# Second mixer: query and forget transposes and all decay levels moved two units up, key copies taken ahead of the exponentials

## The reference, cut to what matters

```python
proj = h @ w_in[i]
da_q, da_k, da_v, hg_q, hg_zf, hg_zb, hg_v, hg_g = split(proj)
# differential attention, 4 heads, two score maps per head
a = softmax(einsum('bqhmd,bkhmd->bhmqk', q * scale, k))
w = a[:, :, 0] - lam * a[:, :, 1]
o_da = rmsnorm_2(einsum('bhqk,bkhe->bqhe', w, v), subln_g) * (1 - lambda_init)
# recurrence, forwards and backwards, 4 heads of 128
log_f = log(lb + (1 - lb) * sigmoid(z))
k_in = (1 - lb) * sigmoid(-z)
state = exp(sum of log_f) * state + k_in^T v ; y = q state
o_hg = rmsnorm_2(y_forward + y_backward, norm_g) * silu(g)
x = x + concat([o_da, o_hg]) @ w_out[i]
```

## Time and profile before

| | us |
|---|---|
| median of 3 runs | 959.13 |
| lowest and highest | 958.48, 961.9 |
| the profiled execution's own time | 959.75 |
| its span | 957.9 |
| TensorE busy | 916.5 (96%) |
| VectorE, ScalarE, GpSimd busy | 593.1, 492.6, 115.7 |
| mean granted TensorE clock | 0.988 of full speed |

### The profile page before, as it was taken

How to read it: one execution, slowest core, us unless ns; L and a number is a source line. 1 busy time by engine, 2 the same in 40 slices (tenths; PEclk the granted TensorE clock), 3 DMA queues, 4 the chain that set the end, 5 groups by cost and what they waited for, 6 DMA issues and landing times.

```text
span 957.9 us, 14230 instructions
## 1 busy us (share of the span) xinstructions
PE 916.5 (96%) x4869; PEld 772.0 (81%) x4869; DVE 593.1 (62%) x882; ACT 492.6 (51%) x729; POOL 115.7 (12%) x107
## 2 busy tenths in 40 slices
PE   7999999999999899999999999997999999999996
PEld 5788888888787677888888878786778999999875
DVE  5655555568756546654555557887666666757664
ACT  6444444465754546444444456554636544545463
POOL 5210000020033202000000021632002000000020
PEclk9999999999999999999999999998999999999998
DMA  9796666447722223655555627441245665555611
GB/s 312 205 266 201 216 191 217 141 129 242 241 68 70 85 69 129 220 186 192 191 186 186 190 75 263 128 140 62 66 129 169 198 196 180 180 192 173 196 45 44
DMA packets 122040, 157.43 MB, mean 164 GB/s; under 512 B 10047, under 2 KB 83011, under 8 KB 122000
## 3 DMA queue, kind: packets, MB, share of 16 engines
q1 hardware_dynamic: 119648, 151.65, 49.6%
q0 software_dynamic: 1904, 4.65, 1.9%
q10 hardware_dynamic: 448, 0.59, 0.2%
HBM read 155.79 MB, written 1.07 MB: 164 GB/s over the span
## 4 chain that ended last, share of the span: by engine, by line
PE 86%; DVE 8%; ACT 3%; issue 2%; DMA 1%; SPq 0%; DVEq 0%; ACTq 0%
PE bank L475 22%; PE bank L477 21%; PE bank L476 21%; PE bank L505 4%; PE bank L507 4%; PE bank L506 4%; DVE w_lo L1664 2%; PE bank L1034 1%; ACT w_hi L1169 1%; PE bank L587 1%; PE bank L688 1%; PE bank L858 1%; PE bank L856 1%; PE bank L866 1%; DMA w_raw<-in_w_ffn_up 1%
## 5 line engine op out<-in xcount | busy, mean ns | idle before, releaser
L1671 DVE TENSOR_TENSOR w_lo<-w_raw,w_hi 128x1024 fp32r<-128x1024 f32 x180 | 220.2, 1224 | 177.4 <-ACT w_hi L1178 177.4
L1178 ACT ACTIVATE w_hi<-w_raw 128x1024 fp32r<-128x1024 f32 x180 | 190.3, 1058 | 210.5 <-PE bank L477 173.9
L475 PE MATMUL bank<-w_hi,x_hi 128*128 128x512 f32 (+1 forms) x688 | 277.8, 404 | 10.9 <-DVE w_lo L1664 2.3
L477 PE MATMUL bank<-w_hi,x_lo 128*128 128x512 f32 (+1 forms) x688 | 268.9, 391 | 0.0
L476 PE MATMUL bank<-w_lo,x_hi 128*128 128x512 f32 (+1 forms) x688 | 268.7, 391 | 0.0
L475 PEld LDWEIGHTS bank<-w_hi,x_hi 128*128 128x128 f32 x688 | 130.6, 190 | 46.4 <-issue 9.5
L1664 DVE TENSOR_TENSOR w_lo<-w_raw,w_hi 128x1024 fp32r<-128x1024 f32 x97 | 120.7, 1271 | 53.4 <-ACT w_hi L1169 52.7
L477 PEld LDWEIGHTS bank<-w_hi,x_lo 128*128 128x128 f32 x688 | 130.4, 190 | 27.8
L476 PEld LDWEIGHTS bank<-w_lo,x_hi 128*128 128x128 f32 x688 | 130.9, 190 | 23.9
L1169 ACT ACTIVATE w_hi<-w_raw 128x1024 fp32r<-128x1024 f32 x108 | 112.1, 1055 | 45.5 <-PE bank L477 41.8
L475 PE MATMUL bank<-w_hi,h_hi 128*128 128x512 f32 (+1 forms) x304 | 116.7, 384 | 4.9 <-DVE h_lo L1830 2.5
(11 more groups left out here) (294 smaller groups left out, 922.1 us busy)
## 6 DMA issues: line engine op xcount, KB each, us to landing
w_raw<-in_w_ffn_gate SPq DMA_DIRECT2D x132, 256.0 KB, 2.9
w_raw<-in_w_ffn_up SPq DMA_DIRECT2D x132, 256.0 KB, 3.1
w_raw<-in_w_ffn_down SPq DMA_DIRECT2D x132, 256.0 KB, 2.9
w_raw<-in_w_in SPq DMA_DIRECT2D x104, 256.0 KB, 3.1
w_raw<-in_w_out SPq DMA_DIRECT2D x32, 256.0 KB, 3.4
w_raw<-in_w_ple_gate SPq DMA_DIRECT2D x16, 256.0 KB, 3.4
arena<-bias_rows POOLq DMA_DIRECT2D x8, 256.0 KB, 4.5
w_raw<-in_cmp_w_k SPq DMA_DIRECT2D x8, 256.0 KB, 4.7
```

The costliest lines, as they stand in the source:

```text
L475: pe.matmul(out_, hi, wh, start=start, stop=False)
L477: return pe.matmul(out_, lo, wh, start=False, stop=stop)
L1178: act.activation(whi[:, slot * UNIT:(slot + 1) * UNIT], raw[:, slot * UNIT:(slot + 1) * UNIT], ACT.Copy).then_inc(sem("hi_done"), 1)
L1671: dve.tensor_tensor(wlo[:, s_], raw[:, s_], whi[:, s_].bitcast(F32), ALU.subtract).then_inc(sem("lo_done"), 1)
```

## The change

Nine things move; the work is the same, and no operation is added or removed.

1. `T2_AT`: the transposes of query and forget tiles follow units (1, 0), (1, 1), (2, 0), (2, 1), (3, 0), (3, 1) instead of the units two later.
2. `hg_prepare` on VectorE is called at step (3, 1) instead of (3, 3).
3. Levels: 0 and 1 at (4, 0), 2 and 3 at (4, 1), then one at each unit from (4, 2) to (5, 3), two at each unit of pass 6.
4. `key_mix` is done ahead: the copies for levels 2 and 3 at step (3, 3), that for level n + 2 at the step of level n, behind that step's split and ahead of its exponentials.
5. The keys' growth on VectorE is a function of its own, `grow_keys(n)`, called ahead of the step's remainder `w_lo` (L1664) instead of behind it.
6. `hg_out` follows unit (7, 0) instead of (7, 1); `across` and `quad_squares(0)` move up by one step with it.
7. `quad_sums(0)` moves from step (7, 2) to (7, 1), `quad_root(0)` with it; on VectorE the six operations of `quad_sums` to `da_weights(3)` are reordered so that `quad_gain(0)` stands ahead of `da_weights(3)`.
8. On ScalarE `staged2(p)` stands ahead of `same_place` and the key copies.
9. GpSimd grows the keys of levels 1 and 2 ahead of the second rotation, where it grew only level 1's.

```diff
--- before.py
+++ after.py
@@ -280,7 +280,7 @@
 
 
         BANKS2 = [(4, 5) if p_ in (1, 3) else (0, 1) for p_ in range(8)]
-        T2_AT = {(1, 2): (0, 0), (1, 3): (1, 0), (2, 2): (2, 1), (2, 3): (3, 1), (3, 2): (4, 2), (3, 3): (5, 2),
+        T2_AT = {(1, 0): (0, 0), (1, 1): (1, 0), (2, 0): (2, 1), (2, 1): (3, 1), (3, 0): (4, 2), (3, 1): (5, 2),
                  (5, 0): (6, 3), (5, 1): (7, 3), (5, 2): (8, 4), (5, 3): (9, 4)}
         STG2_AT = {0: 0, 1: 1, 2: 0, 3: 1, 4: 0}
         STG2_FREE = {0: 0, 1: 0, 2: 2, 3: 4, 4: 6}
@@ -290,14 +290,8 @@
 
         QUAD_SQ = ((cv[:, :], sg[:, :]), (av(DE, [512]), av(DE + 512, [512])))
 
-        def levels_at(p, j):
-
-            if p < 4:
-                return ()
-            if p < 6:
-                return ((), (), (0, 1), (2, 3))[j] if p == 4 else (4 + j,)
-            k = 4 * (p - 6) + j
-            return (8 + 2 * k, 9 + 2 * k) if k < 5 else ()
+        LEVELS_AT = {(4, 0): (0, 1), (4, 1): (2, 3), (4, 2): (4,), (4, 3): (5,), (5, 0): (6,), (5, 1): (7,),
+                     (5, 2): (8,), (5, 3): (9,), (6, 0): (10, 11), (6, 1): (12, 13), (6, 2): (14, 15), (6, 3): (16, 17)}
 
         def both_ways(off, n, h):
 
@@ -1105,11 +1099,11 @@
                     k_unit(u % RING, j, BANKS2[p])
                     if (p, j) in T2_AT:
                         tgroup2(*T2_AT[p, j])
-                    for n in levels_at(p, j):
+                    for n in LEVELS_AT.get((p, j), ()):
                         level(n)
                     if p >= 6:
                         k = 4 * (p - 6) + j
-                        if k == 5:
+                        if k == 4:
                             hg_out()
                         if k % 2 == 0:
                             da_scores(k // 2)
@@ -1571,23 +1565,28 @@
 
             for p in range(8):
                 for j in range(4):
-                    if (p, j) == (4, 3):
-                        same_place(0)
-                        same_place(1)
-                    for n in levels_at(p, j):
-                        key_mix(n)
                     if j == 3:
                         staged2(p)
+                    if (p, j) == (7, 1):
+                        quad_root(0)
                     if (p, j) == (7, 2):
-                        quad_root(0)
                         da_exp(3)
                     split(U_IN2 + 4 * p + j + RING)
                     if p in (2, 3, 5) and (p, j) in T2_AT:
                         g = T2_AT[p, j][0]
                         sigmoids(g) if p < 5 else turned2(g)
+                    if (p, j) == (3, 3):
+                        key_mix(2)
+                        key_mix(3)
+                    if (p, j) == (4, 0):
+                        same_place(0)
+                        same_place(1)
+                    for n in LEVELS_AT.get((p, j), ()):
+                        if n >= 2:
+                            key_mix(n + 2)
                     if p >= 6:
                         k = 4 * (p - 6) + j
-                        if k == 4:
+                        if k == 3:
                             across(0)
                             across(1)
                         if k in (0, 2, 4):
@@ -2286,16 +2285,7 @@
                     return
                 h = 1 << (L - 1)
                 if n == 2:
-                    dve.wait_ge(sem("hq_init"), 1)
-                    dve.wait_ge(sem("t_prod"), 6)
-                    dve.wait_ge(sem("k_done"), 8)
                     dve.wait_ge(sem("con3_in"), 16)
-                if pr == 0:
-                    if L >= 2:
-                        dve.wait_ge(sem("grown_k"), L - 1)
-                    dve.wait_ge(sem("kmix_done"), n - 1)
-                    dve.tensor_tensor(grown(HK, 0, h), grown(HK, 0, h), growth(0, h, True), ALU.mult
-                                      ).then_inc(sem("grown_k"), 1)
                 dve.wait_ge(sem("lv_full"), n + 1)
                 if L >= 2:
                     dve.wait_ge(sem("grown_dve"), 2 * (L - 2) + pr + 1)
@@ -2309,6 +2299,22 @@
                                     raw_ap(con, C_ALL, C_LEVEL + (L - 1) * P, [[0, 2], [0, 2], [1, P]]).bitcast(I32),
                                     bank[4 + pr][:, :].rearrange("p (a b c) -> p a b c", a=2, b=2)
                                     ).then_inc(sem("at_done"), 1)
+
+            def grow_keys(n):
+
+                L = n // 2
+                if n % 2 or not 1 <= L <= 7:
+                    return
+                h = 1 << (L - 1)
+                if L == 1:
+                    dve.wait_ge(sem("hq_init"), 1)
+                    dve.wait_ge(sem("t_prod"), 6)
+                    dve.wait_ge(sem("ksum_done"), 1)
+                else:
+                    dve.wait_ge(sem("grown_k"), L - 1)
+                dve.wait_ge(sem("kmix_done"), n - 1)
+                dve.tensor_tensor(grown(HK, 0, h), grown(HK, 0, h), growth(0, h, True), ALU.mult
+                                  ).then_inc(sem("grown_k"), 1)
 
             def da_max(h):
                 for i in range(2):
@@ -2392,19 +2398,22 @@
                         da_weights(k // 2)
                     if j == 3:
                         staged2(p)
+                    if k == 5:
+                        quad_sums(0)
                     if k == 6:
-                        quad_sums(0)
                         da_max(3)
                         quad_scale(0)
+                        quad_gain(0)
                         da_weights(3)
-                        quad_gain(0)
+                    for n in LEVELS_AT.get((p, j), ()):
+                        grow_keys(n)
                     split(U_IN2 + 4 * p + j + RING)
                     if p < 4 and (p, j) in T2_AT:
                         g = T2_AT[p, j][0]
                         turned2(g) if p == 1 else forget(g)
-                    if (p, j) == (3, 3):
+                    if (p, j) == (3, 1):
                         hg_prepare()
-                    for n in levels_at(p, j):
+                    for n in LEVELS_AT.get((p, j), ()):
                         level(n)
                     if k in (0, 2, 4):
                         da_max(k // 2)
@@ -2554,8 +2563,9 @@
                                    ).then_inc(sem("grown_pool"), 1)
             rotate(0, 3)
             grow(1)
+            grow(2)
             rotate(1, 4)
-            for L in range(2, 8):
+            for L in range(3, 8):
                 grow(L)
             pool.wait_ge(sem("vec_in"), 32)
             for m in range(M):
```

## The result

The changed kernel takes 968.37 us at the median (967.1 to 969.38, 5 runs), the kernel before 959.13. The ratio is 1.0077, with a 95% interval of 1.0052 to 1.0102: slower by 0.8%, outside the range that was forecast. The profiled execution has a span of 966.0 us, 8.1 more than before; 0.9 us of that stand ahead of the second mixer, where the code is the same and two single executions differ. Medians and ratios in this text leave out three executions in a slower state (1522 us of the kernel before, 970 and 2527 us of the kernel with the preparation split).

A forecast was written before the change was run, and what follows sets the result against it. TensorE, busy 96%, was taken as the bound, so only its waits and slow clock could yield. Terms +5.5 + 2.6 - 2.0 - 0.9 - 7.0 - 0.9 + 2.1 = -0.6, plus 1.1, on 959.13 gave 960.2, stated 960.0; range 954.5 to 964.5 us.

The forecast's parts named there:

- item 1: Transposes and `hg_prepare` two units up: transposes cost the same 0.46 us a group, inputs ready one unit before, keys' sum not late.
- Item 2: Level 0, behind unit (4, 0): a new TensorE wait of 5.5 us (4.9 to 6.0) for VectorE's staging behind `hg_prepare`.
- Item 3: After the wait at level 0: the clock certainly falls to half speed, losing 2.6 us (1.7 to 3.3).
- Item 4: Same stretch, passes 4 and 5: the wait of unit (5, 0) goes, -2.0 us; levels 2 and 3 give back -0.9.
- Item 5: Pass 6: levels no longer wait, weights' transposes wait 1.4 and 1.1 us, -7.0 us; unit (7, 0) at full speed, -0.9.
- Item 6: Pass 7, reordered: +1.3 us of new wait for head 2's weights, +0.4 for head 3's scores, +0.4 around (7, 3); sum +2.1.
- The fall of the clock expected behind it: Pass 7, behind the 2.4 us wait in (7, 3): the clock falls once, +1.1 us.
- Rival B: Short waits of the second mixer: each costs the clock, 5.1 us more, 965.1 us; decides from two falls on, 963.4; chance 17%.
- A: Passes 6 and 7: the short waits and the clock's last fall don't arise, 7.1 us less, 952.9 us; chance 15%.
- C: Level 0: the wait doesn't arise, as staging is out sooner, 8.1 us less, 951.9 us; chance 3%.

## Why the prediction was wrong

*The step that failed* is the sentence in item 1, "The transposes cost TensorE the same 0.46 us a group wherever they stand, and their inputs are copied out one unit before." Its first half is right. The second was taken from the loop, where staging stands at the last step of each pass, and not looked up in the timeline for pass 0, where VectorE comes out of the block's norm late and has 3.5 us of remainders ahead of the staging. So the sum had nothing for a wait in pass 1. What the runs show in its place is 6.4 us of wait and 1.7 at half clock, less 0.8 for a remainder's wait that stood there before: 7.3 of the 8.4 us by which 968.37 lies above the forecast of 960.0. Two experiments give 7.0 by the medians (968.37 to 961.36, and 960.67 to 967.66), and 7.9 and 5.8 by the ratios (1.0077 to 0.9995, and 1.006). It wasn't among the rivals either: all three spoke of passes 4 to 7.

*Item 1, rest, right.* `hg_prepare` ran two units sooner; the keys' sum was not late.

*Item 2, right in kind, too large.* 4.4 us instead of 5.5, under the lower bound of 4.9. The preparation ran 7.8 us instead of 8.55, as its last products had no rotation beside them, and part of the rest is that I counted from the last dispatch and the profile from the last matmul's end.

*Item 3, right.* 3.0 us lost at half speed against 2.6, in the profiled execution; with the query transposes put back the same wait lost 1.4.

*Item 4, half right.* No wait in front of (5, 0) (-2.0). But levels 2 and 3 still took 2.82 us at 627.38, the same as before: the 0.9 us did not come back.

*Item 5, right in kind, too large a gain.* From the levels at 656.99 to unit (7, 0) at 680.47 is 23.5 us, not 21.5: -5.0 instead of -7.0. The waits for weights are near what I worked out (1.33 and 0.73 for 1.4 and 1.1), and the work without waits took 19.9 us, not 18.9. Missed were 0.52 and 1.02 us in front of the second level of units (6, 0) and (6, 2), for the masked copy. VectorE's query growth took 1.57 and 1.72 us there instead of 0.68, beside a GpSimd product of the same size, once the keys' growth and once a scaling of the gate:

```profile
656.20 1.57 DVE L2292 TENSOR_TENSOR arena<-arena,sg 128x512 f32<-128x512 f32 x1
...
669.65 1.72 DVE L2292 TENSOR_TENSOR arena<-arena,sg 128x512 f32<-128x512 f32 x1
```

```profile
656.11 1.11 POOL L2562 TENSOR_TENSOR arena<-arena,sg 128x512 f32<-128x512 f32 x1 [8.12 <-ACT arena L1549]
...
669.54 2.94 POOL L2574 TENSOR_TENSOR arena<-arena,hb 128x512 f32<-128x512 f32 x2
```

The unit (7, 0) had full speed.

*Item 6, right.* 1.18 us in (7, 1) for 1.3, 2.09 in (7, 3) for 2.4. The fall of the clock expected behind it came in three of the five profiled executions that have this wait, not in the changed kernel's. It came in that of the kernel with the query transposes put back, whose median is 961.36, where the forecast's own sum, which had nothing for pass 1, gives 961.8 on the 960.7 of that session. That the two are so near is luck in part: item 2 was 1.1 too dark and the clock at level 0 lost less there, items 4 and 5 were 0.9 and 2.0 too hopeful.

*Rival B* doesn't show in the changed kernel, whose short waits left the clock alone in the profiled execution. In the variants it was partly at work: by the account above, more falls of the clock and a longer wait left the key copies alone worth 3.4 us at the median instead of 7. *Rivals A and C* fell: the short waits and the one at level 0 stand in the changed kernel's trace.

## What to carry to other kernels

When an operation is moved up by two steps wherever it occurs, check its first occurrence by itself: at a seam between two stages the producer's queue is another one, and the row to look for is the producer's end beside the consumer's start. A gap of 0.06 us there says that the step has no room to move. A piece of 8 us on an engine whose results are wanted every 3 us made TensorE wait in each of the three places tried. Splitting it, so that what is wanted soonest doesn't queue behind the rest, gave the lowest median (957.7 us against 959.5 and 961.4 for the whole piece in two places), though the intervals overlap.

## What the runs showed of the hardware

The same wait of 4.4 us at level 0 was followed by half speed until 2.9 us after its end with the query transposes back (614.17 to 617.05) and with pass 7 in its old order (613.08 to 615.98), and until 5.9 and 6.1 us after it with the staging first and in the changed kernel (619.88 to 625.96). TensorE's stretches with the query transposes back:

```profile
616.00:617.00 1.00, 1.00 (x7) 0.50 0.84 199
617.00:618.00 1.00, 1.00 (x8) 0.97 0.86 299
```

A wait of 2.06 us in front of unit (5, 0) left the clock alone in the kernel before and with the query transposes moved, and 2.08 us in the same place took it to half speed with the key copies ahead. So a price for one wait of some 2 to 4 us can't be read from one execution; it is a range, here 0 to 3 us beside the wait itself. Ten to twelve executions of one kernel spread over 5.1 to 7.5 us, and their granted clock goes with it: with pass 7 in its old order, 955.33 us at 0.994 and 962.35 at 0.985. Part of that lies outside the mixer: near 332 us, where the code is the same, the profiled executions spent 3.4 us, 10.2 or none at half speed.

A subtraction of 128x1024 on VectorE took 1.23 us alone and 3.43 beside an addition of 128x1024 on GpSimd (3.88 us), and the product of that size 1.48 without it (with small rotation products on GpSimd instead) and 3.42 beside it. Each ended 1.08 us after the addition's end, so this looks like a wait for that end rather than a slower pace, though no run separates the two. It cost 2 us to whichever operation VectorE had in that stretch. The Trainium skill, "GPSIMD Engine Reference", section 8, names this contention for instructions with two SBUF inputs. The traces agree and give its size.
